# A Hymba-style decoder layer on eight cores: another order of the first products, of the second tile's loads and of the weight sums

## The reference

```python
def rms_norm(x, g):
    x32 = x.astype(jnp.float32)
    inv = lax.rsqrt(jnp.mean(x32 * x32, axis=-1, keepdims=True) + EPS)
    return (x32 * inv * g.astype(jnp.float32)).astype(x.dtype)

def swiglu(h, w_gate, w_up, w_down):
    return (jax.nn.silu(h @ w_gate) * (h @ w_up)) @ w_down

# reference(), DEPTH = 1, D_FF = 2816
x = x + 0.5 * swiglu(rms_norm(x, ffn1_norm[l]), ffn1_w_gate[l], ffn1_w_up[l], ffn1_w_down[l])
h = rms_norm(x, mix_norm[l])
z = h @ w_in[l]                                          # (B,S,IN_COLS)
q, k, v, u, gate_b, gate_c = jnp.split(z, IN_SPLITS, axis=-1)
attn = sliding_window_sink_attention(q, k, v, attn_sinks[l], rel_bias_table)
conv = gate_b * causal_short_conv(gate_c * u, conv_w[l])  # (B,S,CONV_DIM)
mixed = jnp.concatenate([rms_norm(attn, attn_out_norm[l]),
                         rms_norm(conv, conv_out_norm[l])], axis=-1)
x = x + mixed @ w_out[l]
x = x + 0.5 * swiglu(rms_norm(x, ffn2_norm[l]), ffn2_w_gate[l], ffn2_w_up[l], ffn2_w_down[l])
return rms_norm(x, final_norm)
```

## Time and profile before

| | |
|---|---|
| three runs | 1185.70, 1186.92 and 1325.98 us, median 1186.92 |
| profiled execution, its own time | 1184.09 us |
| its span, slowest core (core 4) | 1182.5 us (others 1176.8 to 1182.0) |
| TensorE / VectorE / ScalarE busy | 1113.6 / 738.0 / 477.8 us |
| mean granted TensorE clock | 0.993 of full on core 4 |

### The profile page before, as it was taken

How to read it: one execution, slowest core, us unless ns; L and a number is a source line. 1 busy time by engine, 2 the same in 40 slices (tenths; PEclk the granted TensorE clock), 3 DMA queues, 4 the chain that set the end, 5 groups by cost and what they waited for, 6 DMA issues and landing times.

```text
span 1182.5 us, 18174 instructions; the slowest of 8 cores (1176.8 to 1182.5 us)
## 1 busy us (share of the span) xinstructions
PE 1113.6 (94%) x5954; PEld 522.5 (44%) x5954; DVE 738.0 (62%) x1343; ACT 477.8 (40%) x823; POOL 98.6 (8%) x182
## 2 busy tenths in 40 slices
PE   3899999999988999999999999999999899999996
PEld 0455555555444434444443444444444343444444
DVE  2465667545574677767573778773567467675945
ACT  4334442123464445454414454311356544544112
POOL 1000001002000001011010101100100001010110
PEclk9999999999999999999999999999999999999998
DMA  7553334738421339537346566763951135454553
GB/s 182 99 105 72 73 72 64 168 50 146 86 37 19 54 71 219 103 72 111 50 81 110 97 138 121 142 154 61 156 94 19 19 55 102 77 93 82 81 95 146
DMA packets 36858, 111.62 MB, mean 94 GB/s; under 512 B 3616, under 2 KB 13984, under 8 KB 36000
## 3 DMA queue, kind: packets, MB, share of 16 engines
q0 software_dynamic: 31584, 88.62, 43.9%
q1 hardware_dynamic: 4752, 20.78, 5.1%
q10 hardware_dynamic: 432, 1.07, 0.3%
HBM read 190.67 MB, written 8.39 MB: 168 GB/s over the span
## 4 chain that ended last, share of the span: by engine, by line
PE 81%; DVE 7%; issue 4%; DMA 4%; ACT 3%; DVEq 0%; SPq 0%; ACTq 0%; POOL 0%; POOLq 0%
PE psall L588 38%; PE psall L890 15%; PE psall L1088 9%; PE psall L600 5%; PE psall L1404 4%; PE psall L834 3%; DMA w_sb<-wf 2%; PE psall L553 2%; PE psall L709 2%; DMA x_sb<-xs 1%; DVE w_sb L379 1%; PE psall L911 1%; DMA w_sb<-wm 1%; DVE T_sb L816 1%; PE psall L1127 1%
## 5 line engine op out<-in xcount | busy, mean ns | idle before, releaser
L588 PE MATMUL psall<-hq_sb,w_sb 128*128 128x512 bf16 x1248 | 283.8, 379 | 2.2 <-DVE w_sb L379 1.5
L588 PE MATMUL psall<-ht_sb,w_sb 128*128 128x512 bf16 x936 | 215.8, 379 | 7.4 <-DVE w_sb L379 7.4
L379 DVE TENSOR_TENSOR w_sb<-w_sb 128x512 bf16<-128x512 bf16 (+1 forms) x456 | 176.1, 414 | 23.7 <-DMA w_sb<-wf 4.0
L588 PEld LDWEIGHTS psall<-hq_sb,w_sb 128*128 128x128 bf16 x1248 | 120.5, 98 | 152.8 <-issue 11.7
L519 DVE TENSOR_TENSOR u_sb<-psall,u_sb 128x512 f32<-128x512 f32 x156 | 107.6, 691 | 115.4 <-PE psall L588 109.8
L362 POOL DMA_DIRECT2D w_sb<-wf x148 | 82.8, 561 | 944.0 <-DVE a_sb L530 289.8
L546 ACT ACTIVATE sq_sb<-x_sb 128x512 bf16<-128x512 f32 x110 | 66.7, 627 | 192.3 <-DVE x_sb L720 144.2
L588 PEld LDWEIGHTS psall<-ht_sb,w_sb 128*128 128x128 bf16 x936 | 89.8, 98 | 119.1 <-issue 15.4
L516 ACT ACTIVATE u_sb<-psall 128x512 f32<-128x512 f32 x156 | 93.1, 597 | 121.5 <-PE psall L588 106.5
L1088 PE MATMUL psall<-hq_sb,w_sb 128*128 128x512 bf16 x544 | 126.6, 383 | 5.9 <-ACT uS_sb L1171 2.9
L890 PE MATMUL psall<-a_sb,w_sb 128*128 128x512 bf16 x528 | 122.3, 379 | 1.7 <-DVE x_sb L720 1.7
(11 more groups left out here) (103 smaller groups left out, 911.4 us busy)
## 6 DMA issues: line engine op xcount, KB each, us to landing
w_sb<-wf POOLq DMA_DIRECT2D x128, 512.0 KB, 6.5
w_sb<-wm POOLq DMA_DIRECT2D x16, 768.0 KB, 14.8
outT<-x_sb SPq DMA_DIRECT2D x16, 512.0 KB, 4.3
w_sb<-wf POOLq DMA_DIRECT2D x20, 384.0 KB, 8.0
x_sb<-xs SPq DMA_DIRECT2D x2, 2048.0 KB, 20.4
x_sb<-xs SPq DMA_DIRECT2D x6, 512.0 KB, 14.9
eb_sb<-biasT SPq DMA_DIRECT2D x2, 1024.0 KB, 6.3
mk_sb<-maskT SPq DMA_DIRECT2D x2, 1024.0 KB, 11.0
```

The costliest lines, as they stand in the source:

```text
L379: S.op("dve", lambda e: e.tensor_tensor(out=w[:, o, 0:c], in0=w[:, i0, 0:c], in1=w[:, i1, 0:c], op=op), reads=[w.k(i0, slice(0, c)), w.k(i ...
L588: inst = e.matmul(ps[b], lhsT=w[:, wi, c * 128:(c + 1) * 128], rhs=h_op(which, c)[0], start=(start and c == 0), stop=(c == 3), skip_group_ ...
```

## The change

In the first FFN the products of pairs 0 and 1 on tile 0 come first, then those on tile 1, then the halo's products of both pairs, one after the other. Tile 1 of x is loaded later: its first two quarters wait for the last quarter of tile 0 (`toks[3]`), the other two for the first weight. The first weight waits for the third quarter of tile 0 (`toks[2]`), the halo's rows for the third weight. `lead_mid_first` is cut into six steps that are called between products: squares of tile 1, its statistics and multiplies, the halo's, and `setup2` last. In all FFNs `w_sums` takes a list of weights and queues the sums by index, 4 of each, 5 of each, then (`last`) the differences, then 6 of each; `need` asks for one index. The first stage's bias and mask are loaded in pair 5 of the first FFN and not in its down stage.

```diff
--- before.py
+++ after.py
@@ -379,14 +379,18 @@
             S.op("dve", lambda e: e.tensor_tensor(out=w[:, o, 0:c], in0=w[:, i0, 0:c], in1=w[:, i1, 0:c], op=op),
                  reads=[w.k(i0, slice(0, c)), w.k(i1, slice(0, c))], writes=[w.k(o, slice(0, c))])
 
-        def w_sums(n, last=True):
-
-            assert n < st_["issued"]
-            later(("w", n), lambda: w_add(n, 4, 2, 3, ALU.add))
-            later(("w", n), lambda: w_add(n, 5, 4, 0, ALU.subtract))
-            later(("w", n), lambda: w_add(n, 6, 1, 5, ALU.subtract))
+        def w_sums(ns_, last=True):
+
+            for n in ns_:
+                assert n < st_["issued"]
+                later(("w", 4, n), lambda n=n: w_add(n, 4, 2, 3, ALU.add))
+            for n in ns_:
+                later(("w", 5, n), lambda n=n: w_add(n, 5, 4, 0, ALU.subtract))
             if last:
-                w_s3(n)
+                for n in ns_:
+                    w_s3(n)
+            for n in ns_:
+                later(("w", 6, n), lambda n=n: w_add(n, 6, 1, 5, ALU.subtract))
 
         def w_s3(n):
             later(("w3", n), lambda: w_add(n, 2, 0, 2, ALU.subtract))
@@ -411,7 +415,7 @@
 
         def w_early(n):
             early.add(n)
-            w_sums(n)
+            w_sums([n])
 
         def drain_low(k):
             for _ in range(k):
@@ -579,7 +583,7 @@
                         need(("h", 1))
                     need(("t", {3: 0, 4: 4, 5: 1, 6: 2, 7: 3}[P]))
                 if wi >= 4:
-                    need(("w", n))
+                    need(("w", wi, n))
                 if wi == 2:
                     need(("w3", n))
 
@@ -683,10 +687,14 @@
             def fin_pair(j):
                 release(2)
 
-            def plain_t(j, ng, nu, t):
+            def nop_():
+                return None
+
+            def plain_t(j, ng, nu, t, hook=(nop_, nop_)):
                 need(("h", t))
                 for fh in range(2):
                     gplain(ng, fh, fh, t)
+                    hook[fh]()
                     gplain(nu, 3 + fh, fh, t)
                     plain_out(j, fh, t, fh, 3 + fh)
                     drain(3)
@@ -741,21 +749,21 @@
             def ahead(j):
 
                 if j < NPAIR:
-                    for n in (base + 2 * j, base + 2 * j + 1):
-                        if n not in early:
-                            w_sums(n, not has_halo)
+                    w_sums([n for n in (base + 2 * j, base + 2 * j + 1) if n not in early], not has_halo)
             base = st_["consumed"]
             kind, nlead = lead
             if kind == "plain":
-                plain_t(0, *get(0), 0)
-                plain_t(0, *get(0), 1)
-                lead_mid()
-                plain_t(1, *get(1), 0)
+                lead_mid(0)
+                plain_t(0, *get(0), 0, (nop_, lambda: lead_mid(1)))
+                lead_mid(2)
+                plain_t(1, *get(1), 0, (lambda: lead_mid(3), nop_))
+                plain_t(0, *get(0), 1, (nop_, lambda: lead_mid(4)))
+                ahead(nlead)
+                plain_t(1, *get(1), 1)
                 halo_gu(0, *get(0))
                 fin_pair(0)
-                plain_t(1, *get(1), 1)
                 bg.extend(h_sums()[3:4])
-                ahead(nlead)
+                lead_mid(5)
                 halo_gu(1, *get(1))
                 fin_pair(1)
             else:
@@ -918,8 +926,7 @@
                     reads=[PB(b), xh.k(dp), xh.k(dp + 4)], writes=[xh.k(dp), xh.k(dp + 4)])
 
             def dsums(dp):
-                for n in range(base + 25 + 3 * dp, base + 28 + 3 * dp):
-                    w_sums(n, not has_halo)
+                w_sums(range(base + 25 + 3 * dp, base + 28 + 3 * dp), not has_halo)
             jobs.extend(pre_jobs)
 
             def first_prod(dp):
@@ -1452,13 +1459,14 @@
         for t in range(2):
             for i in range(4):
                 toks.append(load(x0[:, t, 2 * i:2 * i + 2, :].rearrange("p a b -> p (a b)"), x_d[0, t][:, i * 1024:(i + 1) * 1024],
-                                 xsem[4 * t + i], x0.k(t, slice(2 * i, 2 * i + 2)), "act" if t == 0 and i % 2 == 1 else "sp"))
+                                 xsem[4 * t + i], x0.k(t, slice(2 * i, 2 * i + 2)), "act" if t == 0 and i % 2 == 1 else "sp",
+                                 [] if t == 0 else [toks[3]] if i < 2 else [(wsem[0]["sem"], 16, None)]))
         S.op("pool", lambda e: e.memset(ones[:], 1.0), writes=[ones.k()])
         S.op("pool", lambda e: e.memset(epst[:], EPS), writes=[epst.k()])
         S.op("act", lambda e: e.activation(out=sm[0][:, 8:9], in_=epst[:, 0:1], func=AF.Ln), reads=[epst.k()], writes=[sm[0].k()])
-        gates[0] = [toks[5]]
+        gates[0] = [toks[2]]
         w_issue()
-        load(xh[:].rearrange("p a b -> p (a b)"), xh_d, su["xh"], xh.k(), "sp", [(wsem[1]["sem"], 16, None)])
+        load(xh[:].rearrange("p a b -> p (a b)"), xh_d, su["xh"], xh.k(), "sp", [(wsem[2]["sem"], 16, None)])
         load(identf[:], ident_d, su["ident"], identf.k(), "sp")
         load(gattn[:], gattn_d, su["gattn"], gattn.k(), "sp")
         load(esink[:, :, 0], sinks_d, su["sinks"], esink.k(), "sp")
@@ -1493,17 +1501,26 @@
             rstd_of(b, width(t), 1.0 / D, r)
             return r
 
-        for t in range(2):
-            r = norm_full(x0, t, 6 + t, 2)
-            for kc in range(8):
-                h_mul(x0, kc, t, G_FFN1, r)
-        bg.extend(h_sums()[:3])
-
-        def lead_mid_first():
-            rh = norm_full(None, "h", 6)
-            for kc in range(8):
-                later(("h", "h"), lambda kc=kc: h_mul(None, kc, "h", G_FFN1, rh))
-            setup2()
+        r0 = norm_full(x0, 0, 6, 2)
+        for kc in range(8):
+            h_mul(x0, kc, 0, G_FFN1, r0)
+
+        def lead_mid_first(at):
+            if at < 3:
+                for kc in ((0, 1, 2, 3), (4, 5), (6, 7))[at]:
+                    sq_row(x0, kc, 1)
+            elif at == 3:
+                r = norm_stats(1, 7)
+                for kc in range(8):
+                    later(("h", 1), lambda kc=kc: h_mul(x0, kc, 1, G_FFN1, r))
+                bg.extend(h_sums()[:3])
+                drain(5)
+            elif at == 4:
+                rh = norm_full(None, "h", 6)
+                for kc in range(8):
+                    later(("h", "h"), lambda kc=kc: h_mul(None, kc, "h", G_FFN1, rh))
+            else:
+                setup2()
 
         def fin_mul(st, x, kc, t, r):
             S.op("dve", lambda e: e.scalar_tensor_tensor(out=x[:, t, kc, :], in0=x[:, t, kc, :],
@@ -1541,7 +1558,8 @@
                 return f
 
             def between1(j, st=st):
-                return None
+                if st == 0 and j == 5:
+                    load_bias(0)
             if first:
                 lead1 = ("plain", 2)
                 mid1 = lead_mid_first
@@ -1555,7 +1573,8 @@
 
             def bias_now(st=st):
                 drain_low(99)
-                load_bias(st)
+                if st == 1:
+                    load_bias(st)
             ffn(st, "1", x, lead1, mid1, between1, first, [], nop, stat_done(0, mix_h(0)), stat_done(1, mix_h(1)), bias_now)
             def norm_t1(x=x):
                 sq_step(3)
```

## The result

The changed kernel takes 1197.7 us (median; its runs 1196.9, 1197.7 and 1198.6) against 1186.3 before (1185.7 and 1186.9): ratio 1.0096, interval 1.0067 to 1.0126. The change costs some 11 us, less than 2%, and the time is outside the range of 1180.5 to 1190.5.

A forecast was written before the change was run, and what follows sets the result against it. TensorE, busy 94% of the span, was taken to bound the kernel, so only its idle time and slow clock counted. 1184.09 + 3.2 (head) - 3.9 (sums) + 0.3 = 1183.7, plus 2.83 to the median: 1186.5 us, range 1180.5 to 1190.5.

The forecast's parts named there:

- the landing of the loads: Head: the second tile's halves go out ahead and delay the weights, which land at 21.3, 25.4 and 31.3 us.
- The clock: Head: the second tile's statistics run from 33.0 to 34.8; a clock loss is counted only after product 7's idle, 1.7 us.
- The fall at product 7: Pair 2: after 5.5 us of idle TensorE the clock falls to the 1.2 GHz level, costing 1.7 us (bounds 0 and 3.5).
- From the statistics to the second tile: Head: table switch, logarithm, multiplies and one product of `a_sb` make the second tile ready at 43.8, after statistics ending at 34.8.
- the halo's waits: Head: 1.5 us for the last two halo multiplies, 1.2 us between adjacent halo products of pairs 0 and 1 sharing a bank.
- Product 7: Pair 2: starts 9.8 us behind the third halo product, at 77.0, behind VectorE's ten sums, `hq_sb` sum and thirteen copies.
- forecast + 3.2: Head: it loses 3.2 us; pair 3's halo product starts at 86.5 against 83.27, although the first product starts 4.7 earlier.
- Sums by use: Three FFNs with split pairs: product 5 goes on at once, product 6 waits less; 1.3 us three times, 3.9 us gained.
- pair 3 cost: Split pairs' pair 3: the sum of index 5 comes second behind the last product, 0.1 us late, 0.3 in all.

The follow-up runs named there:

- e4: The changed kernel with the third weight's load, and all behind it in its queue, waiting for the last quarter of x's second tile: 1196.4 us, ratio 1.0086.
- e2: The changed kernel with the loads of x's second tile and the first weight's and halo rows' waits as before: 1192.8 us, ratio 1.0059.
- e3: The changed kernel, but the second half of x's second tile no longer waits for the first weight: 1196.9 us, ratio 1.0091.
- e5: The changed kernel with the identity's copy and twelve diagonals queued in pair 5 of the first FFN, not ahead of product 7's sums: 1197.3 us, ratio 1.0086.
- e1: The kernel before with only the weight sums queued by index, all else as before: 1181.7 us, ratio 0.9964.

## Why the prediction was wrong

**The step that failed** is the landing of the loads: "I take 21.3, 25.4 and 31.3", by which the halves of the second tile go ahead at x's full rate and the weights pay. The weights came at 18.8 or earlier, 25.3 and 29.5, and x, 7 us of load by itself at 302 GB/s, took from 12 to 40. This moved the statistics by 8.3 us (41.32 for 33.0). An upper bound for x could have been worked out: weights land 3.6 to 4.1 us apart, so six of them and x are 24 and 7 us of load; from 11 us on both are done at 42 by this estimate (the last weight was in at 43.5). If x is served evenly with all that is queued beside it, it is in near there. I bounded the weights by x from both sides and never x by the weights, so no rival held a late second tile. e4 and e2 show that it is the weights beside it; e3 that it is not its own wait.

**The clock**: the statistics behind 6.48 us of idle took 3.57 us and not the 1.73 counted: 1.8 not forecast, a consequence of the late tile. The fall at product 7, 1.7, came as forecast.

**From the statistics to the second tile**: right. 41.32 + 3.57 = 44.9, first matmul on its second half 53.9: 9.0, forecast 34.8 to 43.8. A table switch again takes 1.30 (load starts at 44.97, the logarithm at 46.27). So were the halo's waits, 1.53 and 1.33 (1.5 and 1.2).

**Product 7**: right in its mechanism, VectorE's own work, and 1.3 too long: it starts 8.5 us behind the halo's product, forecast 9.8, since ten sums by index take 3.4 us and not 4.46. What the forecast did not have is the second limit right behind the first: on four cores a weight in a slot freed late (e5). It cost nothing in the changed kernel, and hid what the copies cost when they were taken away.

The balance at pair 3's halo: forecast + 3.2; the statistics + 8.3, their clock + 1.8, the halo's products + 0.3, product 7 - 1.3, in sum 12.3; measured 12.3.

**Sums by use**: the second term that failed, though its mechanism is there. The three waits fell to 0.55, 3.6 us won for the 3.9 forecast, and pair 3 cost 0.58 in e1 for 0.3 (nothing in the changed kernel). But the time is the slowest core's, and there the gain did not arrive: the rest is 1088.6 us on core 4 before, 1088.2 on core 4 of the changed kernel and 1088.6 on e1's core 0. On the mean of the cores it is 2.5 us shorter with the change and 3.9 in e1. On e1's core 0, 2.3 stand again in other waits, 2.24, 1.31 and 1.01 for weights at 275, 622 and 633 us where 1.41, 1.18 and 0.55 were, and a new 0.92 for a sum at 678 (692 in the changed kernel, shown below). All waits of that stretch together are 2.7 us less there, but TensorE is busy 2.65 us longer with the same matmuls (1058.32 against 1055.67): twelve of them in the last mixer take 4.44 where they took 2.75. Why the clock fell there is open.

The changed kernel's second wait of the second FFN's pair 2, and the new one; then e1's wait in the mixer and its twelve slow matmuls; then the same twelve before:

```profile
452.34 1.89 PE L592 MATMUL psall<-ht_sb,w_sb 128*128 128x512 bf16 x8 [0.55 <-DVE w_sb L379]
692.36 2.75 PE L592 MATMUL psall<-ht_sb,w_sb 128*128 128x512 bf16 x12 [0.92 <-DVE w_sb L379]
```

```profile
275.26 1.89 PE L1089 MATMUL psall<-hq_sb,w_sb 128*128 128x512 bf16 x8 [2.24 <-DMA w_sb<-wm]
922.70 4.44 PE L1405 MATMUL psall<-mix_sb,w_sb 128*128 128x512 bf16 x12
```

```profile
924.84 2.75 PE L1404 MATMUL psall<-mix_sb,w_sb 128*128 128x512 bf16 x12
```

**Which cause weighs what**, in ratios: sums by index -0.0036, bias 0, old loads back -0.0037, differences and diagonals mended on top -0.0058, the order itself the remaining 0.0037: 0.0132 between e1 and the changed kernel, each step uncertain by 0.001 to 0.003 and taken in this order. Why the order costs what it does was read from timelines; the single waits of it were not tried one by one. That a weight of pair 3 is late on four cores and not on the others is not explained either.

## What to carry to other kernels

When two streams are put side by side, bound each by the other: add up the time that each takes alone, and let the consumer that can't start without its last piece get it at the end of the sum. Before blaming one piece of an in-order engine's queue for a late result, ask of each instruction there both what it costs and what it waits for, back to the release of a buffer: the next limit can stand right behind the first, so that taking the first away shows nothing in the time. Look at every core then, not at the slowest alone. Queue in-place chains of two buffers alternately: with the order by use, which came in the same edit and was not tried apart, this was the whole good of the change.
